# A down-projection in blocks of seven products instead of eight, with sums on GpSimd

## The reference

```python
def conv_ffn(h, buf, w_up, w_conv, b_conv, w_down):
    gate, up = jnp.split(h @ w_up, 2, axis=-1)
    ...
    gc = b_conv + ext[:, 0:s_len] * w_conv[0]
    for i in range(1, CONV_W):
        gc = gc + ext[:, i:i + s_len] * w_conv[i]
    y = (jax.nn.silu(gc) * up) @ w_down
    return y, ext[:, ext.shape[1] - (CONV_W - 1):]
```

## Time and profile before

| | us |
|---|---|
| median of three runs | 3070.96 |
| the profiled execution, its own time | 3073.04 |
| its span, first to last instruction | 3071.2 |
| `conv_down`, first layer, from SP's first issue to TensorE's last matmul | 1243.55 to 1518.77 |
| `conv_down`, second layer, the same | 2787.79 to 3061.89 |
| TensorE busy over the span | 2841.0 |
| DVE busy over the span | 1962.5 |
| GpSimd busy over the span | 176.1 |

### The profile page before, as it was taken

How to read it: one execution, slowest core, us unless ns; L and a number is a source line. 1 busy time by engine, 2 the same in 40 slices (tenths; PEclk the granted TensorE clock), 3 DMA queues, 4 the chain that set the end, 5 groups by cost and what they waited for, 6 DMA issues and landing times. The chain is left out here.

```text
span 3071.2 us, 48809 instructions
## 1 busy us (share of the span) xinstructions
PE 2841.0 (93%) x18477; PEld 2406.1 (78%) x18477; DVE 1962.5 (64%) x3818; ACT 1343.9 (44%) x2724; POOL 176.1 (6%) x240
## 2 busy tenths in 40 slices
PE   8986988998999999799899799999898999997998
PEld 6762555667999999688799567865678999996887
DVE  5438999865766665577631665249757666665777
ACT  5435996552544444212043455358615434432112
POOL 0000223410000000000000231000000000000000
PEclk9996999999999999899999799999999999998999
DMA  4111001021222222542211201110212222224222
GB/s 151 50 32 26 14 14 49 1 84 58 73 68 83 78 71 71 179 172 99 97 49 51 83 2 54 63 66 2 72 64 60 85 78 71 85 64 186 85 92 87
DMA packets 163369, 220.18 MB, mean 72 GB/s; under 512 B 18588, under 2 KB 123668, under 8 KB 163156
## 3 DMA queue, kind: packets, MB, share of 16 engines
q1 hardware_dynamic: 163156, 217.29, 21.1%
HBM read 160.07 MB, written 56.67 MB: 71 GB/s over the span
## 5 line engine op out<-in xcount | busy, mean ns | idle before, releaser
L2447 DVE TENSOR_TENSOR dn_xres<-dn_dn,dn_xres 128x512 f32<-128x512 f32 (+1 forms) x396 | 266.8, 688 | 133.9 <-PE dn_dn L249 123.7
L247 PE MATMUL dn_dn<-dn_whi,dn_ahi 128*128 128x512 f32 x704 | 275.9, 392 | 25.5 <-DVE dn_alo_r L2427 25.5
L248 PE MATMUL dn_dn<-dn_wlo_r,dn_ahi 128*128 128x512 f32 x704 | 275.4, 391 | 0.0
L249 PE MATMUL dn_dn<-dn_whi,dn_alo_r 128*128 128x512 f32 x704 | 275.3, 391 | 0.0
L2215 DVE SCALAR_TENSOR_TENSOR up_cv<-up_G,tap,up_cv 128x1024 f32<-128x1024 f32 (+1 forms) x176 | 130.3, 782 | 142.4 <-ACT up_cv L2148 140.8
L247 PE MATMUL up_x<-up_th,high 128*128 128x272 f32 x704 | 204.7, 291 | 9.7 <-DVE mixed_c_r L2238 4.8
L249 PE MATMUL up_x<-up_th,low_r 128*128 128x272 f32 x704 | 205.3, 292 | 0.0
L247 PE MATMUL up_x<-up_th,up_high 128*128 128x272 f32 x704 | 202.9, 288 | 1.4 <-DVE up_low_r L1835 1.4
L249 PE MATMUL up_x<-up_th,up_low_r 128*128 128x272 f32 x704 | 203.7, 289 | 0.0
L2387 ACT ACTIVATE dn_whi<-dn_wlo 128x2048 fp32r<-128x2048 f32 x22 | 42.2, 1918 | 324.5 <-DMA dn_wlo<-in_w_down_dram 324.5
L247 PEld LDWEIGHTS dn_dn<-dn_whi,dn_ahi 128*128 128x128 f32 x704 | 133.2, 189 | 53.8 <-DVE dn_alo_r L2427 26.1
(11 more groups left out here) (515 smaller groups left out, 8097.7 us busy)
## 6 DMA issues: line engine op xcount, KB each, us to landing
scratch_a<-up_U SPq DMA_DIRECT2D x44, 544.0 KB, 2.7
dn_alo<-scratch_a SPq DMA_DIRECT2D x22, 1088.0 KB, 7.2
low<-in_w_up_dram SPq DMA_DIRECT2D x44, 512.0 KB, 5.2
up_low<-in_w_up_dram SPq DMA_DIRECT2D x44, 512.0 KB, 5.1
dn_wlo<-in_w_down_dram SPq DMA_DIRECT2D x22, 1024.0 KB, 4.9
scratch_att<-out_x SPq DMA_DIRECT2D x16, 512.0 KB, 2.6
dn_xres<-scratch_att SPq DMA_DIRECT2D x4, 1536.0 KB, 15.0
w_d<-in_w_in_odd_dram SPq DMA_DIRECT2D x7, 768.0 KB, 9.8
```

Of the source, the lines that this page charges most:

```text
L247: nc.tensor.matmul(out, lh, rh, start=first, stop=False, skip_group_check=on_top)
L248: nc.tensor.matmul(out, lh, rl, start=False, stop=False, skip_group_check=on_top)
L249: return nc.tensor.matmul(out, ll, rh, start=False, stop=last, skip_group_check=on_top)
L2447: v.tensor_tensor(xs, bank[0:n, :], xs, ALU.add).then_inc(half_added if t == NT else dn_added, 1)
```

## The change

`conv_down` takes four tiles of the contraction at a time instead of two (a chunk `i` of five, CHUNKS), and the last two tiles stay as a step of the old kind. A chunk's prompt part is a product of 2 x 2 blocks: two halves of 512 rows, two halves of the contraction (even and odd tiles), two halves of 512 columns. It is computed by seven block products p1 to p7 in place of eight. Three of the seven take plain blocks of the gated values (p1, p2, p4), four take sums of them (p5, p6, p3, p7); the weights are plain in p1, p2 and p3 and sums in p5, p6, p7 and p4. Each product is 24 matmuls of 512 columns. PSUM is two halves of four banks, X and Y. TensorE takes the products in the order p1, p2, sx, sy, p6, p5, p7, p3, sz, p4, where sx, sy and sz are the sample rows; p1, p6, p7 and p4 pile up in X, p2 and then p5, p3 in Y, and the next product of a half waits until DVE has added the half as it stands to `xres`.

- In `conv_up` GpSimd makes the four sums of gated values for each pair of tiles (128x512 each, L2138 to L2147 of the new kernel), and SP stores them in a new scratch `s` (`store`). `U` is a ring of three instead of two, and ACT waits for GpSimd before it writes to a `U` again.
- In `conv_down` GpSimd makes the four sums of weights of each chunk in place over the raw weights (128x1024 each, L2597 to L2606).
- ACT makes all high parts and DVE all low parts, seven pairs per chunk, each of 128x1024 (`low`, L2615 and L2617). An add is 128x1024 from two banks (L2641).
- SP loads the four blocks of a chunk's weights (512 KB each) when the low parts that read the block before are done, and after them the seven blocks of gated values (512 KB each).
- The rows of the last step go 0, sample, 1, ..., 7; the fetch of the next stage's weights is cut into three parts.

```diff
 conv_up:
+            def store(m):
+                sp.wait_ge(a_done, FROM + m + 1)
+                sp.dma_start(dram["a"][m], U[m % 3][:]).then_inc(a_out[m % 3], 16)
+                if m % 2 and m < NF - 2:
+                    for j in range(4):
+                        sp.wait_ge(pair_summed, FROM + 4 * (m // 2) + j + 1)
+                        sp.dma_start(dram["s"][m // 2, j], sums_of[j % 2][:]).then_inc(s_out[j % 2], 16)
...
+        @block.gpsimd
+            for i in range(NG - 1):
+                pool.wait_ge(a_done, FROM + 2 * i + 2)
+                pool.wait_ge(s_out[0], FROM + 32 * i)
+                g.tensor_tensor(t0, a21, a22, ALU.add).then_inc(pair_summed, 1)
...
 conv_down:
+PLACES = ("p1", "p2", "p6", "p7", "p5", "p3", "p4")
+        def free_after(i, what):
+            return ready_of(i, {"p1": "sy", "p2": "sy", "p5": "sz", "p3": "sz"}[what]) if what in ("p1", "p2", "p5", "p3") \
+                else ready_of(i, what, NB - 1)
...
         def _(sp):
+            def load_w(i, name):
+                if i:
+                    if name == "b11":
+                        sp.wait_ge(summed, FROM + 4 * i)
+                        sp.wait_ge(w_lo_rest, rest_split_of(i - 1, "p6"))
+                    else:
+                        sp.wait_ge(w_lo_rest, rest_split_of(i - 1, {"b12": "p7", "b22": "p3", "b21": "p4"}[name]))
...
+            def load_a(i, what):
+                if i:
+                    sp.wait_ge(ready, free_after(i - 1, what))
...
+            for i in range(1, CHUNKS):
+                for name in ("b12", "b22", "b11", "b21"):
+                    load_w(i, name)
+                a_stored(sp, 4 * (i + 1))
+                sums_stored(sp, 2 * (i + 1))
+                for what in ("p1", "p2", "p6", "p7"):
+                    load_a(i, what)
+                load_sample(i)
+                for what in ("p5", "p3", "p4"):
+                    load_a(i, what)
...
+        @block.gpsimd
+            b11, b12, b21, b22, t1 = (raw[:, j] for j in range(5))
+            for i in range(CHUNKS):
...
+                g.tensor_tensor(t1, b12, b11, ALU.subtract).then_inc(summed, 1)
+                pool.wait_ge(b_in["b22"], FROM + 16 * (i + 1))
+                pool.wait_ge(w_lo, FROM + 2 * i + 1)
+                pool.wait_ge(summed, FROM + 4 * i + 1)
+                g.tensor_tensor(b11, b22, t1, ALU.subtract).then_inc(summed, 1)
+                g.tensor_tensor(b12, b22, b12, ALU.subtract).then_inc(summed, 1)
+                pool.wait_ge(b_in["b21"], FROM + 16 * (i + 1))
+                pool.wait_ge(w_lo, FROM + 2 * i + 2)
+                pool.wait_ge(summed, FROM + 4 * i + 2)
+                g.tensor_tensor(b21, b21, b11, ALU.subtract).then_inc(summed, 1)
...
         def _(dve):
+            low(0, "p1")
+            low(0, "p2")
...
+            low(0, "p6")
+            for i in range(CHUNKS):
+                add(i, "p1")
+                low_sample(i)
+                low(i, "p5")
+                if i == 0:
+                    low(i, "p7")
+                add(i, "p2")
+                add_sample(i, "sx")
+                add_sample(i, "sy")
+                low(i, "p3")
+                add(i, "p6")
+                low(i, "p4")
+                for j, what in enumerate(("p5", "p7", "p3")):
+                    if i + 1 < CHUNKS:
+                        low(i + 1, PLACES[j])
+                    else:
+                        low_plain(j)
+                    add(i, what)
+                add_sample(i, "sz")
+                if i + 1 < CHUNKS:
+                    low(i + 1, "p7")
...
+                add(i, "p4")
...
         def _(pe):
+            def product(i, what):
...
+                    if what == "p5":
+                        pe.wait_ge(added, added_of(i, "sy" if t else "sx"))
+                    if what in ("p6", "p7", "p3", "p4"):
+                        pe.wait_ge(added, added_of(i, {"p6": "p1", "p7": "p6", "p3": "p5", "p4": "p7"}[what], h))
...
+            def sample(i, what):
...
+                pe.wait_ge(added, added_of(i, "p3" if what == "sz" else "p2", 0))
```

More of the change, by code:

```diff
@@ L2070, in conv_up @@
         G = [sb(f"G{s}", [P, CW]) for s in range(2)]
[L2071 removed]
+        U = [sb(f"U{s}", [P, TOK]) for s in range(3)]
+        sums_of = [sb(f"sum{s}", [P, 512]) for s in range(2)]
         cv = sb("cv", [P, TOK])
         tap, st = first["taps"]
[L2074 removed]
+        tail, a_out, s_out = first["tail"], first["a_out"], first["s_out"]
+        pair_summed = sem("pair_summed")
         banks = {x: [[ph.ps(f"{x}{s}{j}") for j in range(2)] for s in range(2)] for x in "xy"}
@@ L2329, in conv_down, with ready_of, added_of @@
             g_in, ssq, rt, rinv, y_ready = sem("g_in"), sem("ssq"), sem("rt"), sem("rinv"), sem("y_ready")
-        whole = 18 * (NG - 1)
         block = ph.block()
+        rows = [0, NT] + list(range(1, NT))
+        def ready_of(i, what, t=0):
+            before = 0
+            for x in WORK_ORDER:
+                if x == what:
+                    break
+                before += 1 if x[0] == "s" else NB
+            return FROM + (7 * NB + 3) * i + before + t + 1
+        def added_of(i, what, half=0):
+            before = 0
+            for x in WORK_ORDER:
+                if x == what:
+                    break
+                before += 1 if x[0] == "s" else 2
+            return FROM + 17 * i + before + half + 1
@@ L2333, in _, with w_low, a_stored, sums_stored @@
+        def w_low(what):
+            j = place(what)
+            return wlow[1][:, j] if j < 4 else wmore[:, j - 4]
+        def a_stored(sp, tiles):
+            for r in range(3):
+                sp.wait_ge(a_out[r], FROM + 16 * len(range(r, tiles, 3)))
+        def sums_stored(sp, pairs):
+            for r in range(2):
+                sp.wait_ge(s_out[r], FROM + 32 * pairs)
         @block.sync
         def _(sp):
[L2335 to L2340, removed]
@@ L2354, in _ @@
                     sp.dma_start(out[name][layer, j].rearrange("(c p) -> c p", p=P), rowbuf[r0:r0 + NF, 0:P]).then_inc(state_out, 16)
[L2355 to L2359, removed]
-            if fetch is not None:
-                sp.wait_ge(dn_added, FROM + whole + 2)
-                sp.dma_start(fetch.x[:], xres[:, 0, :]).then_inc(fetch.x_in, 16)
+            for i in range(1, CHUNKS):
[8 more added lines that the diff above has]
+                    load_a(i, what)
+                if i == 1 and fetch is not None:
+                    for k in range(FAR - 4):
+                        fetch.fetch(sp, k, fetch.homes[k], fetch.soon_in)
@@ L2383, in _, with high_w @@
             s_ = nc.scalar
[L2384 to L2389, removed]
+            def high_w(i, what):
+                if i:
+                    act.wait_ge(ready, free_after(i - 1, what))
+                if what in ("p1", "p2", "p3"):
+                    act.wait_ge(b_in[{"p1": "b11", "p2": "b21", "p3": "b22"}[what]], FROM + 16 * (i + 1))
+                else:
+                    act.wait_ge(summed, FROM + 4 * i + ("p5", "p6", "p7", "p4").index(what) + 1)
+                s_.activation(whigh[:, place(what)], w_source(what), ACT.Copy).then_inc(w_hi, 1)
@@ new lines, in sample @@
+            def sample(i, what):
+                terms = {"sx": [("p1", 0)], "sy": [("p2", 1)], "sz": [("p5", 0), ("p3", 1)]}[what]
+                b = 1 if what == "sy" else 0
+                if what == "sx":
+                    pe.wait_ge(s_lo, FROM + i + 1)
+                pe.wait_ge(added, added_of(i, "p3" if what == "sz" else "p2", 0))
+                n = 2 * len(terms)
+                for j, (of, k, q) in enumerate((of, k, q) for of, k in terms for q in range(2)):
+                    last = stacked_passes(nc, Y[:, b * 512:(b + 1) * 512], stk[:, 2 * q + k, :], operands(of, q), j == 0, j == n - 1)
+                last.then_inc(ready, 1)
```

384 lines of the change are left out of this document (283 added, 101 removed).

## The result

The changed kernel takes 3139.3 us, the median of four runs (3134.5 to 3142.4), against 3071.0 (3070.8 to 3072.8) for the kernel before: the ratio is 1.022, 95% interval 1.0202 to 1.0237. Its first profiled execution took 3134.5 us, a second one (the experiment `again`) 3142.4.

A forecast was written before the change was run, and what follows sets the result against it. It took TensorE's matmuls to set the time mid-stage; conv_down terms of +27.2 and +21.2 us per layer, together +48.4, on the profile's 3073.0 gave 3121, or 3119 in terms of the runs (chance 0.47), range 3064 to 3134.

The forecast's parts named there:

- `conv_up` at 0: In conv_up, GpSimd's sums make DVE up to 3.5 us late, p3 covers 3.0: cost 0, at most 10 us.
- The pause: In a middle conv_down chunk, DVE idles 6.1 us before the low part of p1's values, which SP issues behind b21.
- The waits of TensorE: In a middle chunk, TensorE waits 2.6 us before p3 and 6.3 before sz for DVE's adds; the chunk takes 50.6.
- the clock: A wait of 6.3 us loses TensorE's clock, costing about 2.0 us; five such waits per layer, +10 us.
- The first chunk: First conv_down chunk takes 70.9 us against 63.1 before, cost +7.8 per layer, lost clocks apart.
- the last: Last conv_down chunk, nothing of a next one to load or sum: 47.8 us (+0.6) first layer, 41.8 (-5.4) second.
- What GpSimd adds: In middle chunks, GpSimd sums of 2.24 us hold up DVE's low parts of p2: 50.6 us instead of 48.3.
- rival 3: Still slower: sums also hold up conv_up (+10) or landings exceed 4.9 us (+8 per us): 3133, chance 0.10.
- the walk: One middle conv_down chunk followed through the engines' queues: 48.3 us before GpSimd's effect, against 47.2 for the same work before.
- The mechanism of these sums: In conv_down, GpSimd and DVE exclude each other for an instruction's length when DVE's low part reads two SBUF tensors.
- The end: After the last step, one add of 0.69 us is last instead of the sample row's four adds: -1.4 per layer.

The follow-up runs named there:

- loads_first: Changed kernel with SP issuing the gated values of the next p1 and p2 right behind b12, ahead of b22, b11 and b21: 3098.2 us.
- both: Changed kernel with SP's loads as in loads_first and DVE's adds of p5, p7 and p3 each ahead of the low part before it: 3054.7 us, ratio 0.9948.
- thin_sums: Changed kernel with GpSimd's sums cut to 16 columns, in conv_up after the first pair and conv_down after the first chunk: 3097.6 us.
- ordered2: Changed kernel with the edits of both, DVE's queue reordered further, GpSimd's first chunk sum and conv_up's sums later, two stores a step later: 3033.8 us, ratio 0.9876.

## Where the prediction was right, and where it was wrong

The direction and the mechanism were right: +48 us forecast, +61 in the first trace, +68 in the medians. The size was not, and 3139 lies above the range of 3064 to 3134. What failed are terms of the sum, above all `conv_up` at 0.

- *The pause.* 6.1 us forecast before the low part of p1's values, 6.0 to 7.5 measured in middle chunks, ended by ACT after a DMA, with b21 ahead in SP's queue. ACT began 5.5 us after SP's issue in the chunk shown, where 4.9 was taken. `loads_first` and `both` show that it is this queue.
- *The waits of TensorE.* 2.6 before p3 and 6.3 before sz were forecast, as a chunk of 50.6 plus 2.0 for the clock, 52.6; the traces have 2.2 to 3.8 and 3.1 to 5.8, and chunks of 52.2 to 54.7 (mean 53.2). Where p3 waits longer and runs slower, sz waits less: DVE's chain sets both. The start of sz is what counts: 43.4 us into the chunk forecast, 43.7 measured on the mean, and 2.3 us of lower clock behind it in place of 2.0.
- *The first chunk* (70.9 plus two clocks, 74.9) came at 73.9 and 75.7 in the first trace, the last at 48.1 and 41.7 (47.8 and 41.8 forecast).
- *What GpSimd adds* is the step that failed, in size. Its largest miss is `conv_up`, which the sum has at 0 because the product p3 was to cover DVE's delay, with 10 us as a bound in rival 3. It measured +5.9 us in the first trace and +6.9 in the second: the cover holds behind three pairs of ten and fails by 0.47 us behind seven, and without the sums, or with them in another place, those steps are back at 21.07. The next one is the first sum of a chunk, which the walk does not place: it can hold up the low part of p4, on which b21 hangs, and the two first chunks are then 7.4 us over the forecast together (second trace) in place of 1.0 (first trace). In middle chunks the price of 2.3 per chunk was low as well: a sum of 128x1024 alone takes 2.4 us (2.24 taken), and taking the sums out gave back 4.0, 2.6 on DVE and 1.4 of clock. By the forecast's prices the sums that `thin_sums` leaves out are worth 8 x 2.3 = 18 us; it gave back 41.7.
- *The mechanism of these sums*, one engine kept out for the length of the other's instruction, was as the forecast read it from the earlier trace rows: the low parts take 3.39 us instead of 1.22. The traces agree with the rule of the Trainium skill (SBUF — State Buffer, Who interferes with whom) for low parts, and with its exception for an instruction with one input in SBUF: the adds, whose other input is PSUM, take 2.35 us for two beside a sum and without.
- *The end.* -1.4 was forecast in each layer; it is -1.6 in the first and +0.5 in the second. In the second DVE is a row tile behind TensorE with adds (1.28 for two) and final norm (0.15 and 1.28): the adds of the last row tile start 2.7 us after the last matmul (3122.51), where before the last tile's adds started 0.6 us after it (3061.66).
- *The range.* In the sum's own terms the first trace is 13 us over the forecast of 3121: 5.9 in `conv_up`, 4.1 in the middle chunks, 1.7 at the end, 1.0 in the first chunks and 0.3 in the last ones. Another 6.9 are that the forecast took the profiled run to stand 2.1 us above the median, as before the change, while here it stands 4.8 below; `again` puts most of such a difference in the first chunks. The upper end, 3134, left no room for this: rival 3's own two prices, +10 for `conv_up` and +8 for one us of landing, already make 3137, and not the 3133 that stands there.

Most of the gain of 54.4 us was there to be had: `ordered2` computes all that the changed kernel computes, and is 37 us faster than the kernel before and some 105 faster than the changed one, by the order of the queues and by two waits of GpSimd, one moved and one added.

## What to carry to other kernels

In this kernel fewer matmuls paid only once the queues around them had the adds that free PSUM ahead of the preparation of the next block. Walk one period through DVE's and SP's queues before counting what is removed. Work given to an idle GpSimd was not free where DVE works on two operands in SBUF (3.39 us for 1.22): put it beside DVE's adds from PSUM or its idle time, and look whether a DMA or another engine hangs on the instruction that it can hold up.

## What the runs showed of the hardware

- GpSimd's sum or difference of two float32 tensors took 1.29 us for 128x512 and 2.40 for 128x1024 when undisturbed. The Trainium skill (GPSIMD Engine Reference, section 3.1) has 4497 ns for an add of 2048 columns; a quarter and half of it, 1.12 and 2.25 us as estimates, are 13% and 6% below what the traces have.
- After a wait the clock can fall late. In the middle chunk shown in the section on the result, stretches in the columns of the earlier trace rows:

```profile
1354.20:1359.40 5.20, 5.20 (x12) 4.08 (x13) 5.20 (x3) 2.60 (x3) 4.51 (x2) 0.50 0.00 0
1360.20:1362.30 2.10, 2.10 (x11) 1.69 (x9) 2.10 (x3) 0.61 (x1) 2.10 (x1) 1.00 0.00 0
1362.80:1365.00 2.20, 0.00 (x0) 0.00 (x0) 2.20 (x3) 0.00 (x0) 0.00 (x0) 1.00 0.02 4
1367.00:1370.20 3.20, 3.20 (x9) 2.51 (x8) 1.64 (x2) 0.00 (x0) 0.00 (x0) 0.50 0.14 33
```

The first two are p3, behind its wait of 3.4 us: 0.50 (1.2 GHz) at first, then 1.00. The other two are the wait of 3.1 us before sz and the matmuls behind it: 1.00 through the wait, and 0.50 among the matmuls that came after. In this chunk the slower matmuls (0.43 us apart instead of 0.23) cost 2.9 us behind the wait before p3 and 1.8 behind that before sz, beyond the waits' own length. Behind the waits of 3.1 to 5.8 us before sz in the six middle chunks of this trace they cost 1.6 to 2.9.
